# Two modulation sums of each feed-forward moved behind its down product, on one core

## The chip, the cores and the metric

The kernel runs on one core of one Trainium2 chip. The metric is the device time of one execution in microseconds (us), as the median of several runs. PE is TensorE, DVE is VectorE, ACT is ScalarE, POOL is GpSimd, SP is SyncE; PEld is PE's loading of weights.

## What is computed

Two transformer blocks of two layers each over 256 tokens of width 1024, all in float32. Cut to what matters here:

```python
def first_block(x, ...):
    for i in range(2):
        h = rms_norm(x, norm_mix_w[i])
        ...                                       # i = 0: gated delta rule; i = 1: nsa attention
        x = x + concatenate([mix, mo]) @ w_out[i]
        x = x + conv_glu(rms_norm(x, norm_ffn_w[i]), ffn_w_up[i], ..., ffn_w_down[i])
    return rms_norm(x, final_norm_w)

def second_block(x, c, w_ada, b_ada, ...):
    cond = silu(c)
    for l in range(2):
        mod = cond @ w_ada[l] + b_ada[l]          # 1024 -> 6144
        shift1, scale1, gate1, shift2, scale2, gate2 = split(mod, 6)
        h = rms_norm_2(x, norm1_g[l]) * (1 + scale1) + shift1
        ...                                       # mLSTM and attention mixers
        x = x + gate1 * (merged @ w_out[l])
        h2 = rms_norm_2(x, norm2_g[l]) * (1 + scale2) + shift2
        x = x + gate2 * hierarchical_moe(h2, ...) # 32 experts
```

The modulations `mod` of the second block depend on `c` alone, so they can be made while the first block runs. Each of the two layers has 12 chunks of 512 columns; the kernel numbers them 0 to 23.

## The kernel before

**Engines and order.** Every engine has its own program, written out by hand as a function (`sync`, `tensor`, `vector`, `scalar`, `gpsimd`), in which `gdn`, `project_out(0)`, `ffn(0)`, `nsa`, `project_out(1)`, `ffn(1)`, and twice `mixers` and `moe` follow one another. An engine runs its program in that order; semaphores tie the engines together.

**Weights.** SP asks for weight blocks of 2 MB (some of 1 MB) in a fixed order. They go to `wring`, a ring `W` of five places (more in the expert stage). A request waits until the block that held its place before has been freed, and those behind it wait too. Around each down product SP's order is: down block, chunk 3 (or 18), down block, chunk 4 (19), down block, chunks 5 and 6 (20 and 21), down block, chunks 7 and 8 (22 and 23), and two last down blocks; then the blocks of the next stage. With five places, the place of chunk 7 goes to the second block of the next stage and that of chunk 8 to the third, which in the first feed-forward is chunk 9 (`ADA_NSA`, line 526). The first block of the next stage takes the place of the down block ahead of them.

**One modulation chunk.** `ada_chunk` (VectorE, L120 and L129) multiplies the block's eight tiles by `silu(c)` and adds them up in the block's first tile, in eight instructions. `ada_sum` (PE, L106) adds over the 128 partitions by one product of 128x512 with a matrix of ones (tiles `ps<-wring,CS`; two records in the trace) into a bank of the ring `PB`, and frees the weight place. `ada_out` (VectorE) takes the result out of the bank and frees it: four instructions for a scale (L125, L137, L129, L125), three for a shift, one for a gate (L125, `AR<-ps,AR`). Chunks 7 and 8 are a half of `scale2` and a half of `shift1`; 22 and 23 are the halves of layer 1's `gate2`.

**Banks.** PSUM has eight banks: the ring `PA` is `ps0` to `ps3`, the ring `PB` is `ps4` to `ps7`. `bank` takes the next place of a ring in turn and waits until what was in it has been read.

**The down product.** `down` (line 718) makes 256x1024 results in four banks of `PA` (token half m, column half c). Five groups of weight blocks follow one another, the last made of two blocks; PE waits for both before it starts it. Behind each of the first four groups stands what `between` gives, here the sums of `ADA_DOWN`:

```python
    ADA_DOWN = [[(3,), (4,), (5, 6), (7, 8)], [(18,), (19,), (20, 21), (22, 23)]]
```

**The norm behind it.** VectorE adds each result to X (`add_x`), makes the statistics of each token half with ACT's help and writes XN (`norm_part`). PE transposes XN by halves (`norm_half`, L109: four transposes into each of two banks of `PB`). The scaled transposes go to HT: the first token half by ACT alone, of the second half four features by VectorE (`norm_features`) and four by ACT. In the first feed-forward ACT scales a half as soon as it is there (`norm_ends`); in the second it first makes the roots of two norms for both halves, since a final norm of the first block lies between, and then scales both halves. Only then `features` (PE) multiplies the next stage's weights with HT.

In the first feed-forward the transposes of token half 0 stand inside `down`, ahead of its last quarter (`then` is "nsa"), and those of half 1 at the start of `nsa`. In the second one both stand at the start of `mixers(0)` (lines 1230 and 1231 before).

Of the kernel before, what the change touches and what calls it, by code (L numbers as in the profile page):

```python
# [294 lines left out]
def build(nc, t, out):  # L295
# [98 lines left out]
    G = at(10752, 22, 256)  # L394
# [130 lines left out]
    ADA_DOWN = [[(3,), (4,), (5, 6), (7, 8)], [(18,), (19,), (20, 21), (22, 23)]]  # L525
# [148 lines left out]
    def tensor(e):  # L674
# [43 lines left out]
        def down(done, tag, srcs, lhs, between=(), then=None, ready=(), halfway=None):  # L718


            groups = [[x] for x in srcs[:-2]] + [srcs[-2:]]
            for n, group in enumerate(groups):
                held = [(weights(name, kt, 1024), k0, kt) for name, k0, kt in group]
                final = n == len(groups) - 1
                for m in range(2):
                    if n == 0 and m and halfway:
                        halfway()
                    for c in range(2):
                        if n == 0:
                            bank(e, PA, (tag, m, c))  # L730
                        if final and m and c and then:
                            norm_half(then, 0)
                        for i, (wt, k0, kt) in enumerate(held):
                            if ready:
                                e.wait_ge(*ready[n + i])
                            for k in range(kt):
                                ins = e.matmul(PA[tag, m, c][:, :], lhs[:, k0 + k, tok(m)], wt[:, k, c * 512:c * 512 + 512],
                                               n == 0 and i == 0 and k == 0, final and i == len(held) - 1 and k == kt - 1)
                        if final:
                            ins.then_inc(done, (tag, m, c))  # L740
                if not final:
                    ins.then_inc(done, (tag, "group", n))
                for name, _, _ in group:
                    W.free(name, (done, (tag, 1, 1) if final else (tag, "group", n)))
                if n < len(between):
                    between[n]()
# [310 lines left out]
        def ffn(layer):  # L1057

            done, vect = sig("ffn_mm"), sig("ffn_v")
            tag = ("ffn", layer)  # L1060

            def product(i, part):
                name, nb = up_name(layer, i), up_blocks(i)
                a11, a12, a21, a22, total = up_tiles(layer, i)
                if part == 1:
                    bank(e, PB, ("p1", name))
                    place(name)
                    lhs, rhs, to = a11, HT[:, 0:4, tok(0)], (PB["p1", name], 0)
                    e.wait_ge(sig("norm_ha"), (tag, 0, 3))
                elif part == 2:  # L1070
                    bank(e, PA, ("p26", name))
                    lhs, rhs, to = a12, HT[:, 4:8, tok(0)], (PA["p26", name], 0)
                    e.wait_ge(sig("norm_ha"), (tag, 0, 7))
                elif part == 7:
                    bank(e, PA, ("p57", name))
                    lhs, rhs, to = a21, TS[2], (PA["p57", name], nb)
                    e.wait_ge(vect, ("t", layer, 2))
                    e.wait_ge(vect, ("s3", name))
                elif part == 5:
                    lhs, rhs, to = total, TS[0], (PA["p57", name], 0)  # L1080
                    e.wait_ge(vect, ("t", layer, 0))
                    e.wait_ge(vect, ("s1", name))
                elif part == 6:
                    lhs, rhs, to = a11, TS[1], (PA["p26", name], nb)
                    e.wait_ge(vect, ("t", layer, 1))
                    e.wait_ge(vect, ("s2", name))
                elif part == 3:
                    bank(e, PA, ("p34", name))
                    lhs, rhs, to = a12, HT[:, 4:8, tok(1)], (PA["p34", name], 0)
                    e.wait_ge(sig("norm_ha"), (tag, 1, 7))  # L1090
                    e.wait_ge(vect, ("s4", name))
                else:
                    lhs, rhs, to = a22, TS[3], (PA["p34", name], nb)
                    e.wait_ge(vect, ("t", layer, 3))
                ps, b0 = to
                for b in range(nb):
                    for k in range(4):
                        c = 128 * (b0 + b)
                        ins = e.matmul(ps[:, c:c + 128], lhs[:, k, 128 * b:128 * b + 128], rhs[:, k, :], k == 0, k == 3)
                ins.then_inc(done, (name, part))  # L1100
                if part == 4:
                    W.free(name, (done, (name, 4)))
                elif part == 5:
                    SUMS.free(name, (done, (name, 5)))

            product(0, 1)
            product(0, 2)
            norm_half(tag, 1)
            for i, part in ((1, 1), (1, 2), (0, 7), (0, 5), (0, 6), (0, 3), (0, 4), (1, 7), (1, 5), (1, 6)):
                product(i, part)  # L1110
            PA.defer()
            product(1, 3)
            product(1, 4)
            for i in range(2, 12):
                for part in (1, 2, 7, 5, 6, 3, 4):
                    product(i, part)
                if i - 1 in ADA_UP[layer]:
                    ada_sum(ADA_UP[layer][i - 1])

            srcs = [(("down", layer, j), 4 * (j - 1) if j else 20, 4 if j else 2) for j in DOWNS]  # L1120
            ready = [(vect, ("val", layer, j - 1 if j else 5)) for j in DOWNS]
            down(done, tag, srcs, G, [lambda ns=ns: [ada_sum(n) for n in ns] for ns in ADA_DOWN[layer]],
                 None if layer else "nsa", ready)

        def nsa():
            done, vect, act = sig("nsa_mm"), sig("nsa_v"), sig("nsa_a")
# [100 lines left out]
        def mixers(layer):  # L1227
            done, vect, act = sig(f"mix_mm{layer}"), sig(f"mix_v{layer}"), sig(f"mix_a{layer}")
            tag = ("mix", layer)
            norm_half(tag, 0)  # L1230
            norm_half(tag, 1)
            for ch in range(2):
                name = (f"qk{ch}", layer)
# [348 lines left out]
    def vector(v):  # L1582
# [409 lines left out]
        def ffn(layer):  # L1992
            done, mm, act = sig("ffn_v"), sig("ffn_mm"), sig("ffn_a")
            tag = ("ffn", layer)
# [97 lines left out]
            for n in range(first, last + 2):  # L2092
                if n <= last:
                    ada_chunk(n)
                if n > first:
                    ada_out(n - 1)
            for m in add_x(mm, tag, done):
                if layer:
# [3 lines left out]
                    norm_part("nsa", m)  # L2102
            if layer == 0:
                norm_features("nsa")

        def last_part(tag, m):
            r, f = norm_scale(tag, m)
# [94 lines left out]
        def mixers(layer):  # L2202
            done, mm, act = sig(f"mix_v{layer}"), sig(f"mix_mm{layer}"), sig(f"mix_a{layer}")
            tag = ("mix", layer)
            norm_features(tag)
            RAW, E, S3 = mixer_rings(layer)
            lg, e1, neg, nb, cb = (sm((n, layer), 2, 8) for n in ("lg", "me1", "neg", "nb", "cb"))
            halves = lambda x: x.rearrange("p a (b c) -> p a b c", b=2)
# [998 lines left out]
```

## Time and profile before

| what | value |
|---|---|
| median of 3 runs | 2495.95 us (2493.03 to 2497.18) |
| the profiled execution | 2493.57 us |
| its span, first to last instruction | 2491.8 us |
| PE busy | 2239.1 us (90%) |
| DVE busy | 1085.4 us (44%) |
| ACT busy | 588.3 us (24%) |
| DMA, mean rate | 261 GB/s |
| mean granted clock of PE | 0.958 |

The profile shows one execution. Times in it count from the start of its span. PE's busy time overlaps from one matmul to the next, and the ends of matmuls are modelled; where PE waits is read from the idle time ahead of a row. The first feed-forward's down product runs from 502 to 586 us, the second's from 980 to 1064 us; the experts of the second block run from about 1320 on, with a mixer stage of the second layer between 1780 and 2025.

### The profile page before, as it was taken

To read this page: it belongs to the slowest core of one execution; us is meant where nothing else is said; L and a number is where in the kernel's file an instruction comes from. 1 tells how busy PE (TensorE), PEld (TensorE's weight loads), DVE (VectorE), ACT (ScalarE), POOL (GpSimd) and SP (SyncE) were. 2 spreads that over 40 slices of the span, in tenths; PEclk is the share of its full clock that TensorE was granted. 3 is DMA by queue.
4 is the path that set the end of the run, shared out by engine and by line. 5 is a ranking of instruction groups with operands and counts; after the bars stand their busy time and mean duration, and the time that the engine had idled before them with its cause. 6 is when DMAs were issued, how large, how long until landed. Compare 5 with 4: busy or idle time off the path is not lost.

```text
span 2491.8 us, 31934 instructions
## 1 busy us (share of the span) xinstructions
PE 2239.1 (90%) x12996; PEld 1463.1 (59%) x12996; DVE 1085.4 (44%) x2397; ACT 588.3 (24%) x1304; POOL 58.4 (2%) x88
## 2 busy tenths in 40 slices
PE   8999999899989999999998977877899989887886
PEld 7888879846865798467763433333568744333332
DVE  4764458873464787543433222222324342222222
ACT  4331423001143220032522111111214421111111
POOL 0010000001000000002000000000002000000000
PEclk9999999999999999999998999999899989999998
DMA  7221234586932645835248999999743369999996
GB/s 277 102 77 68 102 133 169 189 335 193 318 123 99 223 170 210 330 130 169 102 184 361 427 428 427 427 428 427 294 150 115 158 264 427 427 427 427 427 427 286
DMA packets 140910, 651.37 MB, mean 261 GB/s; under 512 B 6971, under 2 KB 13419, under 8 KB 116049
## 3 DMA queue, kind: packets, MB, share of 16 engines
q1 hardware_dynamic: 138336, 642.19, 65.4%
q0 software_dynamic: 2416, 7.02, 1.2%
q8 instruction: 106, 1.74, 0.3%
q14 instruction: 52, 0.42, 0.0%
HBM read 647.88 MB, written 1.31 MB: 261 GB/s over the span
## 4 chain that ended last, share of the span: by engine, by line
PE 62%; DMA 23%; DVE 10%; ACT 3%; issue 2%; DVEq 0%; ACTq 0%
PE ps L106 60%; DMA wring<-in_w_up 13%; DMA AR<-in_w_up 8%; DVE AR L125 2%; PE ps L109 2%; DVE AR L129 2%; DMA wring<-in_ffn_w_down 1%; DVE wring L129 1%; ACT AR L115 1%; DVE wring L125 1%; ACT L115 1%; DVE AR L120 1%; ACT HT L115 1%; DVE AR L133 0%; ACT wring L115 0%
## 5 line engine op out<-in xcount | busy, mean ns | idle before, releaser
L106 PE MATMUL ps<-HT,wring 128*128 128x256 f32 (+1 forms) x2848 | 533.6, 346 | 10.7 <-DVE wring L125 9.2
L106 PEld LDWEIGHTS ps<-HT,wring 128*128 128x128 f32 x2848 | 468.5, 194 | 68.1 <-DVE wring L125 11.0
L106 PE MATMUL ps<-wring,AR 128*32 128x512 f32 (+3 forms) x1344 | 338.1, 599 | 18.1 <-DVE AR L125 14.1
L106 PE MATMUL ps<-wring,MN 128*32 128x512 f32 (+1 forms) x1408 | 220.7, 636 | 59.5 <-DMA wring<-in_w_up 39.2
L115 ACT ACTIVATE AR<-ps 128x128 f32<-128x128 f32 (+6 forms) x234 | 94.5, 404 | 719.5 <-PE ps L106 663.1
L106 PEld LDWEIGHTS ps<-wring,AR 128*32 128x32 f32 (+1 forms) x1344 | 132.6, 149 | 176.4 <-issue 173.6
L106 PE MATMUL ps<-AR 128*128 128x128 f32 (+7 forms) x1432 | 204.6, 416 | 15.5 <-DVE AR L125 13.1
L125 DVE TENSOR_TENSOR AR<-ps,AR 128x512 f32<-128x512 f32 (+4 forms) x200 | 100.6, 503 | 264.5 <-ACT AR L115 165.3
L106 PEld LDWEIGHTS ps<-wring,MN 128*32 128x32 f32 (+1 forms) x1408 | 65.3, 122 | 210.9 <-issue 100.3
L141 DVE COPY HT<-ps 128x512 f32<-128x512 f32 x64 | 44.3, 692 | 326.2 <-PE ps L106 326.2
L106 PEld LDWEIGHTS ps<-AR 128*128 128x128 f32 (+5 forms) x1432 | 139.2, 173 | 54.7 <-issue 41.7
L106 PE MATMUL ps<-AR,MN 128*32 128x512 f32 (+1 forms) x800 | 107.7, 650 | 45.5 <-DMA AR<-in_w_up 40.5
L106 PEld LDWEIGHTS ps<-CS,HT 128*128 128x128 f32 x1024 | 119.1, 191 | 48.9 <-issue 48.9
L115 ACT ACTIVATE HT<-ps 128x512 f32<-128x512 f32 x112 | 66.9, 597 | 311.8 <-PE ps L106 310.3
L106 PE MATMUL ps<-XN,wring 128*128 128x128 f32 x1056 | 133.3, 280 | 6.3 <-DVE wring L125 6.3
L106 PEld LDWEIGHTS ps<-XN,wring 128*128 128x128 f32 x1056 | 126.9, 196 | 6.9 <-DVE wring L125 6.8
L129 DVE SCALAR_TENSOR_TENSOR wring<-wring,CC 128x512 f32<-128x512 f32 x168 | 126.3, 752 | 6.0
L106 PE MATMUL ps<-CS,HT 128*128 128x32 f32 x1024 | 126.2, 277 | 0.0
L106 PE MATMUL ps<-XN,AR 128*128 128x128 f32 (+1 forms) x656 | 114.2, 414 | 1.6 <-DVE AR L137 1.6
L106 PEld LDWEIGHTS ps<-AR,MN 128*32 128x32 f32 (+1 forms) x800 | 28.5, 120 | 116.7 <-DMA AR<-in_w_up 56.8
L125 DVE TENSOR_TENSOR MN<-ps,AR 128x512 f32<-128x512 f32 x64 | 44.3, 692 | 119.4 <-PE ps L106 119.4
L115 ACT ACT_TABLE_LOAD x66 | 84.7, 1283 | 13.2 <-issue 5.1
(172 smaller groups left out, 2140.7 us busy)
## 6 DMA issues: line engine op xcount, KB each, us to landing
wring<-in_w_gate SPq DMA_DIRECT2D x40, 2048.0 KB, 37.1
wring<-in_w_up SPq DMA_DIRECT2D x40, 2048.0 KB, 32.0
wring<-in_w_down SPq DMA_DIRECT2D x40, 2048.0 KB, 35.2
wring<-in_w_ada SPq DMA_DIRECT2D x24, 2048.0 KB, 8.5
AR<-in_w_down SPq DMA_DIRECT2D x24, 2048.0 KB, 35.2
AR<-in_w_gate SPq DMA_DIRECT2D x24, 2048.0 KB, 35.5
AR<-in_w_up SPq DMA_DIRECT2D x24, 2048.0 KB, 31.2
wring<-in_ffn_w_up SPq DMA_DIRECT2D x20, 2048.0 KB, 8.0
```

Source lines behind the costliest of these rows:

```text
L106: return Ins(self.eng and self.eng.matmul(out, lhs, rhs, start=start, stop=stop), None)
L109: return Ins(self.eng and self.eng.transpose(out, in_, ident), None)
L115: return Ins(self.eng and self.eng.activation(out, in_, func, **kw), self)
L120: return Ins(self.eng and self.eng.tensor_scalar(out, in_, s1, None, op0), self)
L125: return Ins(self.eng and self.eng.tensor_tensor(out, in0, in1, op), self)
L129: return Ins(self.eng and self.eng.scalar_tensor_tensor(out, in0, s, in1, op0, op1), self)
L141: return Ins(self.eng and self.eng.tensor_copy(out, in_), self)
```

## The change

The sums of the last entry of `ADA_DOWN` (chunks 7 and 8, then 22 and 23) leave the place ahead of the last group of the down product. On PE they now stand behind the whole product, in the first feed-forward ahead of the transposes of token half 1, in the second between the transposes of the two halves. On VectorE `ada_chunk` stays where it was, and `ada_out` of these chunks goes behind `norm_features` of the next stage.

```diff
@@ tensor, ffn(layer)
-            down(done, tag, srcs, G, [lambda ns=ns: [ada_sum(n) for n in ns] for ns in ADA_DOWN[layer]],
+            down(done, tag, srcs, G, [lambda ns=ns: [ada_sum(n) for n in ns] for ns in ADA_DOWN[layer][:3]],
                  None if layer else "nsa", ready)
+            if layer:
+                norm_half(("mix", 0), 0)
+            for n in ADA_DOWN[layer][3]:
+                ada_sum(n)
@@ tensor, mixers(layer)
-            norm_half(tag, 0)
+            if layer:
+                norm_half(tag, 0)
             norm_half(tag, 1)
@@ vector, ffn(layer)
-                if n > first:
+                if n > first and n - 1 not in ADA_DOWN[layer][3]:
                     ada_out(n - 1)
...
             if layer == 0:
                 norm_features("nsa")
+                late_sums(0)
+
+        def late_sums(layer):
+
+            for n in ADA_DOWN[layer][3]:
+                ada_out(n)
@@ vector, mixers(layer)
             norm_features(tag)
+            if layer == 0:
+                late_sums(1)
```

PE in the first feed-forward, before: from the sums ahead of the down product's last group to the first products of the nsa stage. `ps4` to `ps7` are the ring `PB`; `ps<-wring,CS` are the sums; `[waits ...]` names the semaphores.

```order
L106 MATMUL ps6<-wring,CS 128x512 [waits s_ada_v]
L106 MATMUL ps7<-wring,CS 128x512 [waits s_ada_v]
L106 MATMUL ps3<-wring,AR 128x512 [waits s_w2,s_w1]
...
L109 MATMUL ps4<-CS,XN 128x128 [waits s_norm_v]
...
L109 MATMUL ps5<-CS,XN 128x128 [waits s_norm_v]
...
L106 MATMUL ps2<-wring,AR 128x512 x8
L109 MATMUL ps6<-CS,XN 128x128 [waits s_norm_v,s_ada_v]
...
L109 MATMUL ps7<-CS,XN 128x128 [waits s_norm_v,s_ada_v]
...
L106 MATMUL ps4<-HT,wring 128x256 [waits s_norm_ha,s_norm_hv,s_w3]
```

The same stretch of PE in the changed kernel:

```order
L106 MATMUL ps3<-wring,AR 128x512 [waits s_w2,s_w1]
...
L109 MATMUL ps6<-CS,XN 128x128 [waits s_norm_v]
...
L109 MATMUL ps7<-CS,XN 128x128 [waits s_norm_v]
...
L106 MATMUL ps2<-wring,AR 128x512 x8
L106 MATMUL ps4<-wring,CS 128x512 [waits s_ada_v]
L106 MATMUL ps5<-wring,CS 128x512 [waits s_ada_v]
L109 MATMUL ps6<-CS,XN 128x128 [waits s_norm_ha,s_norm_v]
...
L109 MATMUL ps7<-CS,XN 128x128 [waits s_norm_ha,s_norm_v]
...
L106 MATMUL ps4<-HT,wring 128x256 [waits s_norm_hv,s_ada_v,s_w3]
```

The two sums stand behind the last quarter of the down product and hold ps4 and ps5; the first products of the nsa stage take ps4 after sum 7, and wait for s_ada_v, not for the transposes' reader.

VectorE at the same place, from the last scaling of XN on, before:

```order
L121 TENSOR_SCALAR XN<-X,SM 128x512 [waits s_norm_v] x2
L120 TENSOR_SCALAR HT<-ps6,PV 128x128 [waits s_norm_v,s_norm_mm]
L120 TENSOR_SCALAR HT<-ps6,PV 128x128 [waits s_norm_hv] x3
L120 TENSOR_SCALAR AR<-ps6 8x512 [waits s_norm_hv,s_nsa_mm]
L120 TENSOR_SCALAR wring<-wring,CC 128x512 [waits s_nsa_v,s_w0]
```

and in the changed kernel:

```order
L120 TENSOR_SCALAR HT<-ps6,PV 128x128 [waits s_norm_hv] x3
L125 TENSOR_TENSOR ps4<-ps4,CS 64x8x64 [waits s_norm_hv,s_ada_mm]
L137 TENSOR_REDUCE MC<-ps4 64x8 [waits s_ada_v]
L129 SCALAR_TENSOR_TENSOR MC<-MC,PV 64x8 [waits s_ada_v]
L125 TENSOR_TENSOR MC<-MC,PV 64x8 [waits s_ada_v]
L125 TENSOR_TENSOR ps5<-ps5,CS 128x512 [waits s_ada_v,s_ada_mm]
L137 TENSOR_REDUCE MC<-ps5 128x4 [waits s_ada_v]
L125 TENSOR_TENSOR MC<-MC,PV 128x4 [waits s_ada_v]
L120 TENSOR_SCALAR AR<-ps6 8x512 [waits s_ada_v,s_nsa_mm]
```

The seven instructions that empty ps4 and ps5 stand behind the scalings of HT, where they had been ahead of the additions to X.

PE behind the second feed-forward, before: the transposes of both token halves and the first products of the mixer stage.

```order
L109 MATMUL ps7<-CS,XN 128x128 [waits s_norm_v]
...
L109 MATMUL ps4<-CS,XN 128x128 [waits s_norm_v]
...
L109 MATMUL ps5<-CS,XN 128x128 [waits s_norm_v,s_ada_v]
...
L109 MATMUL ps6<-CS,XN 128x128 [waits s_norm_v,s_ada_v]
...
L106 MATMUL ps7<-HT,wring 128x256 [waits s_norm_ha,s_norm_hv,s_w1]
```

and in the changed kernel:

```order
L109 MATMUL ps5<-CS,XN 128x128 [waits s_norm_v]
...
L109 MATMUL ps6<-CS,XN 128x128 [waits s_norm_v]
...
L106 MATMUL ps7<-wring,CS 128x512 [waits s_ada_v]
L106 MATMUL ps4<-wring,CS 128x512 [waits s_ada_v]
L109 MATMUL ps5<-CS,XN 128x128 [waits s_norm_ha,s_norm_v]
...
L109 MATMUL ps6<-CS,XN 128x128 [waits s_norm_ha,s_norm_v]
...
L106 MATMUL ps7<-HT,wring 128x256 [waits s_norm_hv,s_ada_v,s_w1]
```

The transposes of the second half now follow those of the first in the same two banks, and wait for s_norm_ha, ACT's scalings; the first products take the bank of sum 22.

## Rows read from the trace of the kernel before

**Rows 1.** The page's part 4: the chain that ended last, shares of the span.

```profile
PE 62%; DMA 23%; DVE 10%; ACT 3%; issue 2%; DVEq 0%; ACTq 0%
```

**Rows 2.** The chain in order of time, 500 to 1160: start us, us, what.

```profile
540.06 17.02 DMA wring<-in_ffn_w_down
...
590.17 91.36 PE ps L106 x522
...
1071.45 88.64 PE ps L106 x366
```

**Rows 3.** Timeline of PE, first feed-forward: start us, us, what, [idle before].

```profile
553.60 1.02 PE L106 MATMUL ps<-wring,CS 128*128 128x512 f32 x2
555.01 1.12 PE L106 MATMUL ps<-wring,CS 128*128 128x512 f32 x2 [0.39 <-DVE wring L129]
557.21 20.84 PE L106 MATMUL ps<-wring,AR 128*128 128x512 f32 x48 [1.08 <-DMA wring<-in_ffn_w_down]
...
578.76 7.03 PE L106 MATMUL ps<-wring,AR 128*128 128x512 f32 x16
588.96 1.21 PE L109 MATMUL ps<-CS,XN 128*128 128x128 f32 x8 [3.17 <-DVE XN L121]
590.12 15.74 PE L106 MATMUL ps<-HT,wring 128*128 128x256 f32 x64
...
606.74 14.08 PE L106 MATMUL ps<-HT,wring 128*128 128x256 f32 x64
```

**Rows 4.** Timeline of DVE, first feed-forward.

```profile
555.06 0.71 DVE L125 TENSOR_TENSOR ps<-ps,CS 64x512 f32<-64x512 f32 x1
...
556.73 0.16 DVE L125 TENSOR_TENSOR MC<-MC,PV 64x8 f32<-64x8 f32 x1
...
589.62 1.51 DVE L120 TENSOR_SCALAR HT<-ps,PV 128x128 f32<-128x128 f32 x4 [0.23 <-PE ps L109]
...
607.63 0.49 DVE L120 TENSOR_SCALAR wring<-wring,CC 128x512 f32<-128x512 f32 x1
...
613.74 0.49 DVE L120 TENSOR_SCALAR wring<-wring,CC 128x512 f32<-128x512 f32 x1
```

**Rows 5.** Timeline of PE, second feed-forward.

```profile
1031.53 1.88 PE L106 MATMUL ps<-wring,CS 128*128 128x512 f32 x4
1035.16 27.70 PE L106 MATMUL ps<-wring,AR 128*128 128x512 f32 x64 [1.75 <-DMA wring<-in_ffn_w_down]
1062.70 1.04 PE L109 MATMUL ps<-CS,XN 128*128 128x128 f32 x8
1069.51 1.94 PE L109 MATMUL ps<-CS,XN 128*128 128x128 f32 x8 [5.77 <-DVE XN L121]
1071.24 15.85 PE L106 MATMUL ps<-HT,wring 128*128 128x256 f32 x64
```

**Rows 6.** Timeline of DVE, second feed-forward.

```profile
1033.45 0.69 DVE L125 TENSOR_TENSOR AR<-ps,AR 64x512 f32<-64x512 f32 x1 [0.18 <-PE ps L106]
...
1070.63 1.75 DVE L121 TENSOR_SCALAR HT<-ps,MC 128x128 f32<-128x128 f32 x4 [0.69 <-PE ps L109]
```

**Rows 7.** Timeline of ACT, second feed-forward.

```profile
1068.25 5.97 ACT L115 ACTIVATE HT<-ps,MC 128x128 f32<-128x128 f32 x12
```

**Rows 8.** Stretches: busy us (x) of PE, PEld, DVE, ACT, POOL; clock, DMA, GB/s.

```profile
590.30:593.60 3.30, 3.30 (x9) 2.59 (x9) 0.76 (x3) 1.37 (x4) 2.16 (x4) 0.50 1.05 400
593.70:597.00 3.30, 3.30 (x17) 2.91 (x16) 0.00 (x0) 0.00 (x0) 0.00 (x0) 1.00 1.06 359
1071.30:1074.90 3.60, 3.60 (x10) 2.88 (x10) 1.01 (x3) 2.69 (x6) 1.07 (x2) 0.50 0.76 247
```

**Rows 9.** Timeline of SP's requests, first feed-forward.

```profile
553.79 1.23 SPq L101 DMA_DIRECT2D wring<-in_nsa_w_in  x2
...
585.82 0.37 SPq L101 DMA_DIRECT2D wring<-in_nsa_w_in  x1
```

**Rows 10.** Waits of SP's queue, 1140 to 1400: total us, times, longest.

```profile
SPq L101 <- PE ps L106: 229.7, 28, 29.9
```

## The prediction, made before the changed kernel ran

> **What bounds the kernel now.** I read the page first: the chain that ended last is three fifths TensorE [rows 1], so a microsecond saved or lost on PE counts only where the chain runs on PE. The chain in order of time shows where that is around the change [rows 2]. In the first feed-forward it goes through the last load of down weights (17.02 us, from 540.06) and from 590.17 through 522 matmuls in a row; behind the second it takes PE again from 1071.45. A start that is late there moves all that follows. Later the experts' loads end last in the chain, but until they run without a break the SP queue waits for PE, 28 times and 229.7 us between 1140 and 1400 [rows 10]: places in the weight ring come free when PE has read them, so a late PE makes late loads. I therefore pass every PE delay on in full, and take nothing off.
>
> **In front of the last group.** PE's timeline of the first feed-forward [rows 3]: the fourth of five groups ends at about 553.6, the sums of chunks 7 and 8 run from 553.60 and 555.01 with 0.39 us of waiting for VectorE, and then PE waits 1.08 us for a load of in_ffn_w_down and starts the last group at 557.21. The chain says the same [rows 2]: 540.06 + 17.02 = 557.08 is that load, asked for when the sums of chunks 5 and 6 had freed its place. Neither moves. So with two sums fewer PE only waits longer, some 3.6 us (553.60 to 557.21). In the second feed-forward the sums run 1031.53 to 1033.4 and the last group starts at 1035.16, again behind a load [rows 5]. **Gain in front: 0.** The bounds: 0, and 3.6 + 3.6 us if the load came before PE is there. One small way to that exists: the next two weight blocks are asked for at 553.79 [rows 9], 3.3 us before the awaited load lands, and the second of them now goes out only behind the last group. Those requests stand behind the awaited one, so I take 0. The Trainium skill, page "DMA: Bandwidth & Descriptors", section "Two DMAs through the same engine are not ordered", says that within one queue of one DMA engine descriptors start in order but are pipelined and that nothing orders them across the engines; by its first half the gain is 0, by its second a fraction of a microsecond could be there. No row here separates the two.
>
> **Behind the last group, first feed-forward.** PE ends it at 585.79 (578.76 + 7.03) and stands idle 3.17 us until the second half's XN is there at 588.96 [rows 3]. Two sums are four matmul records of 512 columns, each 7.03 / 16 = 0.44 us: 1.8 us. They fit in the idle, and the transposes still start at 588.96. **Cost there: 0**, covered by VectorE's norm of the second half; without that cover it would be the 1.8 us.
>
> The bill comes at the banks. The order of PE shows it: the sums now take two of the four banks of ring PB between the norm's halves, so the first product of the nsa columns gets ps4, the bank of sum 7, and waits for s_ada_v. Before it got the bank of the first half's transposes, which ScalarE had long emptied. VectorE empties the sum's bank in `ada_out(7)`, which now stands behind `norm_features`: 4 scalings from 589.62 take 1.51 us, to 591.13 [rows 4]. `ada_out(7)` took from 555.06 to 556.73 + 0.16 = 556.89, that is 1.83 us with its four instructions, so it ends at 593.0, and PE starts 0.14 us later, at 593.14, not at 590.12 [rows 3, 4]. **+3.0 us.** `ada_out(8)` has no more instructions, so it ends at most 1.9 us later, and its bank is wanted only after half a chunk of products (15.74 / 2 = 7.9 us). VectorE's own work is not late: its next chunk starts at 607.63 [rows 4].
>
> **Second feed-forward.** The transposes of the norm's first half move from `mixers` into `ffn`, to the same place in PE's order; new are the two sums behind them. PE is free at 1063.74, the XN comes at 1069.51 [rows 5]: the sums hide again. But here the transposes of the second half now share ps5 and ps6 with those of the first, and wait for s_norm_ha. ScalarE scales the first half only from 1068.25, because it makes both halves' roots first: 12 scalings in 5.97 us, 0.497 each [rows 7], so ps5 is free at 1068.25 + 4 x 0.497 = 1070.24 and ps6 at 1072.2. The first four transposes go from 1069.51 to 1070.38. VectorE began its scalings 1.12 us after those transposes (1070.63 against 1069.51), so now 1071.5, and ends 1.75 us later [rows 6], at 1073.25. Then `ada_out(22)`, one instruction of 0.69 us [rows 6], to 1073.96; PE starts at 1074.1, not at 1071.24 [rows 5]. **+2.9 us.** ScalarE's four last scalings end near 1075.4, by when PE, at 0.49 us for a k, doesn't need them yet.
>
> **The clock.** The granted clock is 0.50 (the 1.2 GHz level) from about 590.3 to 593.6 and from 1071.3 to 1074.9, and 1.00 right behind the first stretch [rows 8]. Both followed an idle PE, 3.17 and 5.77 us, and both ended 4.7 and 5.4 us after PE's first work (588.96 to about 593.7, 1069.51 to about 1074.9). Products at the lower level cost about 3.4 / 2 = 1.7 us and 3.7 / 2 = 1.85 us. After the change the sums cut the first idle to 1.4 us, but a second one of 3 us follows the transposes, so I expect the lower level again. If the level returns 4.7 and 5.4 us after the products start, instead of after the transposes, the low stretches cost 2.35 and 2.7 us: 0.65 and 0.85 more. If it doesn't fall in the first feed-forward, 1.7 less. I take half of the 1.5: **+0.8**, since part of the earlier return was paid by the transposes; bounds -1.7 and +1.5.
>
> **Loads held back.** The place of chunk 7 goes to the second nsa block and that of chunk 8 to chunk 9. They were asked for at 553.79 and just behind it, the next pair at 585.82 [rows 9]; now all four go out from about 586.8. At 400 GB/s [rows 8] a block of 2.1 MB takes 5.2 us: they land near 592, 597, 603 and 608 with no wait between. PE wants the second block at 606.74, VectorE chunk 9 at 607.63 and chunk 10 at 613.74 [rows 3, 4], all 3 us later by now. Behind the second feed-forward the second block is wanted not before 1087.1 (1071.24 + 15.85) [rows 5]. **0**, with 5 us of cover at the tightest place.
>
> **Sum.** 0 + 3.0 + 2.9 + 0.8 = +6.7 us. Against the profiled execution (2493.57 us, its span 2491.8) that is 2500.3; the median of the three runs is 2.4 us above that execution, so I forecast 2495.95 + 6.7 = 2502.6 us. A measurement of this kernel can tell about 0.2% (5 us) from no change.
>
> **Rivals.**
> 1. *The load comes in time.* Place: the last load of down weights. If with fewer blocks behind it it landed before PE's fourth group ends, PE would gain up to 3.6 + 3.6 = 7.2 us in front, against +6.7: 2495.5, no slower than before. It decides from the point where the wait in front of the last group falls below 3.6 us. Against it: the load is asked for at the same moment, and the wait behind the sums was there in both feed-forwards. A part of it (1 to 2 us) is more likely than all: 0.08.
> 2. *The clock stays up.* The sums break the first idle, the level doesn't fall, and the second stretch costs what it did: 3.0 + 2.9 - 1.7 = +4.2, 2500.2. For it: the longest idle left is no longer than before. Against: two idles close together, with little work between them. 0.10.
> 3. *The banks cost nothing*, so the change moves only idle time: 2496. The Trainium skill, page "Perfetto Trace Analysis", section "Optimizing Tensor Performance", advises that independent matmul groups rotate through banks so that emptying one overlaps the next group's matmuls; by it the waits would be hidden. The order speaks against it: the ring has four places and comes round to the sum's bank before VectorE is at `ada_out`. 0.06.
> 4. *A held-back load is late.* If the four loads took 10 us each, chunk 10 would land near 627, 10 us late, and its sum and the third block with it: at least +5 more, 2508. For it: small loads of GpSimd share that stretch. Against: the rates of rows 8. 0.08.
>
> My forecast itself has 0.68. Its own range is +4.5 to +9; some 0.58 of the 0.68 lies above +5, with rival 4 giving 0.66 for slower. Same takes the rest of the forecast (0.10), rival 2 (0.10), and 0.10 of rivals 1 and 3. Faster is left with 0.04, the far ends of these two. The range from 2497.5 to 2507.0 leaves out the full forms of rivals 1, 3 and 4.
>
> **What would show it.** In the new profile: PE's wait of about 3.6 us in front of the last group, put down to in_ffn_w_down, with the start of the group where it was; the sums right behind the down product; the transposes of the first feed-forward not later; 522 matmuls that start 3 us later behind a wait for VectorE; in the second, transposes that wait for ScalarE's HT in two pieces and products 2.9 us later. It would be wrong if the last group starts sooner by more than 1 us, if the products behind the norm wait less than 2 us more, or if PE waits for in_nsa_w_in or in_w_ada.

## The result, and the profile of the changed kernel

The changed kernel takes 2505.86 us, the median of 6 runs (2503.11 to 2512.66), beside 2494.38 us for the kernel before in the same session (6 runs, 2490.64 to 2497.18): ratio 1.0058, 95% interval 1.0043 to 1.0073. It is 11.5 us slower by the medians (their quotient is 1.0046) and 14.5 by the ratio, with 10.7 to 18.2 in its interval, where +6.7 was forecast. The sign and both bank waits were right; what was missing is the slower last group behind a longer wait, and a further loss between the two feed-forwards.

The execution profiled of the changed kernel is the slowest of its six (2512.66 us), 6.8 us above their median and 19.1 above the profiled one of before. The two feed-forwards are set against those of before by the same landmarks in both traces; of the rest, only whole stretches are compared. The page (its first line, and part 4: shares of the chain that ended last) answers to [rows 1]:

```profile
span 2510.6 us, 31938 instructions
...
PE 64%; DMA 21%; DVE 10%; ACT 3%; issue 2%; DVEq 0%; ACTq 0%
```

PE's part of the chain grew and the transfers' part shrank: the loss sits where PE leads. PE's timeline of the first feed-forward (start us, us busy, instructions; in brackets idle time ahead and what ended it) answers to [rows 3]:

```profile
538.52 13.90 PE L106 MATMUL ps<-wring,AR 128*128 128x512 f32 x32
...
555.54 23.79 PE L106 MATMUL ps<-wring,AR 128*128 128x512 f32 x48 [3.12 <-DMA wring<-in_ffn_w_down]
579.16 1.04 PE L109 MATMUL ps<-CS,XN 128*128 128x128 f32 x8
580.03 7.03 PE L106 MATMUL ps<-wring,AR 128*128 128x512 f32 x16
586.90 1.88 PE L106 MATMUL ps<-wring,CS 128*128 128x512 f32 x4
590.23 1.21 PE L109 MATMUL ps<-CS,XN 128*128 128x128 f32 x8 [1.45 <-DVE XN L121]
...
594.45 16.31 PE L106 MATMUL ps<-HT,wring 128*128 128x256 f32 x64 [3.00 <-DVE MC L125]
611.64 14.08 PE L106 MATMUL ps<-HT,wring 128*128 128x256 f32 x64
```

The 3.00 us in front of the products is the bank wait. But the last group's first 48 records take 23.79 us, where they took 20.84. VectorE's timeline shows who held the bank (answers to [rows 4]):

```profile
590.90 1.51 DVE L120 TENSOR_SCALAR HT<-ps,PV 128x128 f32<-128x128 f32 x4 [0.23 <-PE ps L109]
...
592.51 0.71 DVE L125 TENSOR_TENSOR ps<-ps,CS 64x512 f32<-64x512 f32 x1
...
594.18 0.17 DVE L125 TENSOR_TENSOR MC<-MC,PV 64x8 f32<-64x8 f32 x1
```

It empties sum 7's bank only behind the scalings of HT, and ends at 594.35; PE starts 0.10 us later. PE's timeline of the second feed-forward (answers to [rows 5]):

```profile
1027.40 13.90 PE L106 MATMUL ps<-wring,AR 128*128 128x512 f32 x32
...
1044.83 29.40 PE L106 MATMUL ps<-wring,AR 128*128 128x512 f32 x64 [3.53 <-DMA wring<-in_ffn_w_down]
1074.07 1.04 PE L109 MATMUL ps<-CS,XN 128*128 128x128 f32 x8
1074.94 1.88 PE L106 MATMUL ps<-wring,CS 128*128 128x512 f32 x4
1081.79 1.08 PE L109 MATMUL ps<-CS,XN 128*128 128x128 f32 x4 [4.97 <-ACT HT L115]
1083.82 1.09 PE L109 MATMUL ps<-CS,XN 128*128 128x128 f32 x4 [0.94 <-ACT HT L115]
1085.56 16.51 PE L106 MATMUL ps<-HT,wring 128*128 128x256 f32 x64 [0.65 <-issue]
1101.90 3.64 PE L106 MATMUL ps<-SW,HT 128*128 128x16 f32 x32
```

The transposes wait for ScalarE's HT in two pieces. The first products then wait for sum 22's bank, which VectorE begins to empty only here:

```profile
1084.77 1.48 DVE L125 TENSOR_TENSOR AR<-ps,AR 64x512 f32<-64x512 f32 x2
```

The granted clock in stretches of the changed kernel (stretch; us; busy us of PE, PEld, DVE, ACT, POOL with counts; clock; DMA share; GB/s) answers to [rows 8]:

```profile
552.50:555.40 2.90, 0.00 (x0) 0.00 (x0) 1.08 (x2) 0.00 (x0) 0.00 (x0) 0.87 1.02 388
555.60:560.40 4.80, 4.80 (x6) 2.09 (x7) 0.00 (x0) 0.00 (x0) 0.00 (x0) 0.50 0.89 329
563.00:566.00 3.00, 3.00 (x9) 1.32 (x8) 0.37 (x1) 0.00 (x0) 0.00 (x0) 1.00 0.00 0
1045.00:1048.00 3.00, 3.00 (x6) 1.23 (x6) 0.00 (x0) 0.00 (x0) 0.00 (x0) 0.69 1.04 383
594.50:597.80 3.30, 3.30 (x8) 2.64 (x9) 1.50 (x3) 0.00 (x0) 0.00 (x0) 0.50 1.06 364
```

Behind the longer load wait PE starts the last group at 0.50, the 1.2 GHz level, and is back at 1.00 by 563. Before, with the sums inside that wait, the group started at full speed, as a stretch of the kernel before shows:

```profile
557.30:562.00 4.70, 4.70 (x11) 2.08 (x12) 1.25 (x3) 0.00 (x0) 0.00 (x0) 1.00 1.05 390
```

In the second feed-forward the changed kernel has 0.69 from 1045 to 1048 and 0.74 in the 3 us behind, where the kernel before has 1.00 from 1035.3 to 1040. The ledger between landmarks, us:

| stretch of PE | before | after | difference |
|---|---|---|---|
| first feed-forward: fourth group to last group | 17.34 | 17.02 | -0.32 |
| last group to transposes of token half 2 | 31.75 | 34.69 | **+2.94** |
| transposes to first nsa products | 1.16 | 4.22 | +3.06 |
| products to the second nsa block | 16.62 | 17.19 | +0.57 |
| second feed-forward: fourth group to last group | 17.37 | 17.43 | +0.06 |
| last group to transposes of half 1 | 27.54 | 29.24 | **+1.70** |
| transposes of half 1 to first products | 8.54 | 11.49 | +2.95 |
| products to the small products (128x16) | 15.69 | 16.34 | +0.65 |
| sum | | | +11.6 |

The sum lies within the interval and at the 11.5 of the medians, but it isn't all that the change costs: of the 19.1 us between the two profiled executions it leaves 7.5 elsewhere, 4.7 of them between the two feed-forwards, where the old kernel's work is unchanged. 11.6 and 4.7 make 16.3, which lies in the interval too. So that 11.6 meets the medians doesn't show that nothing else was lost. The 4.7 us: from the second nsa block to the second feed-forward's fourth group it takes 415.76 us, before 411.05. A piece of the same work in both, the changed kernel's stretch first and then that of before:

```profile
690.00:695.00 5.00, 3.89 (x16) 3.33 (x17) 1.40 (x8) 4.54 (x10) 0.00 (x0) 0.62 0.78 285
```

```profile
685.00:690.00 5.00, 3.68 (x22) 3.04 (x23) 2.15 (x13) 4.54 (x9) 0.00 (x0) 1.00 0.77 281
```

Over the next 5 us the clock is 0.70 against 1.00: the level fell here too, 100 us behind the change, and in these 10 us alone 3.4 us of clock are missing. The three kernels whose first feed-forward is as before (the old one, and two of the experiments below) take 411.05, 411.00 and 411.02 us between the feed-forwards; the other eight take 412.2 to 423.7. So an edit in the first feed-forward shows again in this stretch, through the clock as here, in some kernels through waits for loads.

Below, S1 is the sum of the first four lines (66.87 before, 73.12 after), S2 of the last four (69.14 and 74.50).

### The profile page after: what moved, and what is told of

Its sections match the earlier page's. It is cut to its first block, busy times and chain, and to the rows that moved or that the text cites. A ratio compares the mean times of both kernels' runs of the same rounds, so it can differ in the third digit from the quotient of the medians.

```text
span 2510.6 us, 31938 instructions
## 1 busy us (share of the span) xinstructions
PE 2254.3 (90%) x12996; PEld 1471.2 (59%) x12996; DVE 1085.5 (43%) x2397; ACT 588.8 (23%) x1304; POOL 58.4 (2%) x88
## 3 DMA queue, kind: packets, MB, share of 16 engines
q8 instruction: 107, 1.75, 0.3%
## 4 chain that ended last, share of the span: by engine, by line
PE 64%; DMA 21%; DVE 10%; ACT 3%; issue 2%; DVEq 0%; ACTq 0%
PE ps L106 61%; DMA wring<-in_w_up 10%; DMA AR<-in_w_up 9%; DVE AR L125 2%; PE ps L109 2%; DVE AR L129 2%; DMA wring<-in_ffn_w_down 1%; DVE wring L129 1%; ACT AR L115 1%; DVE wring L125 1%; ACT HT L115 1%; ACT L115 1%; DVE AR L120 1%; DVE AR L133 0%; ACT MN L115 0%
## 5 line engine op out<-in xcount | busy, mean ns | idle before, releaser
L106 PE MATMUL ps<-AR 128*128 128x128 f32 (+7 forms) x1432 | 209.4, 424 | 15.2 <-DVE AR L125 12.6
```

Source lines behind the costliest of these rows:

```text
L106: return Ins(self.eng and self.eng.matmul(out, lhs, rhs, start=start, stop=stop), None)
```

## The experiments

Theory: two bank waits of 3 us, and the clock level lost in the last groups. Rivals: the clock follows the new waits behind the norm; the loads that are now asked for late; something elsewhere in the kernel. The kernel before ran again beside each set of experiments, and each median stands beside its own.

**Banks.** The moved sums go to the ring `PA`, idle there, so that no product or transpose comes round to their bank.

```diff
+    LATE = (7, 8, 22, 23)
...
-            ps = bank(e, PB, ("ada", n))
+            ps = bank(e, PA if n in LATE else PB, ("ada", n))
```

> The changed kernel, with the four moved sums in banks of the ring PA, which the down product has just left, instead of PB. Theory: the waits behind the norm come from the ring PB, so the first products of the next stage start behind the transposes again: 3.0 us back in the first feed-forward, and 2.9 us in the second, where the transposes of the second half no longer wait for ScalarE; the slower last group stays. Against the kernel before: +5.5 us (2 to 8). Rival: the waits come from VectorE's later ada_out wherever the sums lie, or from the load traffic that moved there; then the products still start 3 us late and the time stays at +11.5 us.

Measured: 2498.49 against 2491.81 us, ratio 1.0033 [1.0022, 1.0044]. S1 67.77, S2 70.54. PE's timeline of this kernel:

```profile
553.79 23.66 PE L106 MATMUL ps<-wring,AR 128*128 128x512 f32 x48 [3.26 <-DMA wring<-in_ffn_w_down]
...
588.27 1.24 PE L109 MATMUL ps<-CS,XN 128*128 128x128 f32 x8 [1.36 <-DVE XN L121]
589.46 14.05 PE L106 MATMUL ps<-HT,wring 128*128 128x256 f32 x64
...
651.47 1.94 PE L106 MATMUL ps<-wring,CS 128*128 128x512 f32 x2 [3.65 <-DVE MC L125]
```

Both bank waits are gone, and with the first one the low clock behind it; S1 falls by 5.35, S2 by 3.96 (the block behind the small products then takes 1.7 back: 15.75 us, before 14.06). The last group stays slow: its clock has nothing to do with the banks. The time is within the expected range by the medians, and just above it by the ratio (8.2 us). The 0.9 and 1.4 us left in S1 and S2 don't make up the 6.7 us of the medians; between the feed-forwards it takes 416.68 us, 5.6 more than before, and 3.65 of that is the last row, a new wait: VectorE is late with chunk 11's sum. VectorE's timeline, and the chain at the same place (start us, us, what), show what it waits for:

```profile
643.50 0.48 DVE L120 TENSOR_SCALAR wring<-wring,CC 128x512 f32<-128x512 f32 x1 [4.99 <-DMA wring<-in_w_ada]
```

```profile
618.51 24.96 DMA wring<-in_w_ada
```

A load of 2 MB takes 25 us. The stretches of the same kernel, around the place where the held-back loads run and where GpSimd's transfers of bias_rows join them:

```profile
598.00:604.00 6.00, 6.00 (x28) 4.61 (x26) 0.00 (x0) 0.42 (x2) 0.00 (x0) 1.00 1.04 384
622.00:628.00 6.00, 6.00 (x29) 5.30 (x28) 0.16 (x1) 0.77 (x2) 0.00 (x0) 1.00 1.03 164
```

and of the kernel before:

```profile
598.00:604.00 6.00, 6.00 (x30) 5.28 (x29) 0.00 (x0) 0.77 (x2) 0.00 (x0) 1.00 0.18 63
622.00:628.00 6.00, 6.00 (x30) 5.28 (x29) 1.27 (x3) 0.00 (x0) 2.04 (x4) 1.00 1.03 158
```

Before, the share over 598 to 604 was 0.18, with little left to load, so the loads had a start on the slow stretch; here it still runs at full share. That this head start is what is missing is read from the rows; no run moved it alone. In the changed kernel itself VectorE takes chunk 11 at 645.87 without a wait: the late loads are covered by the other delays, and come out when these are mended. The Trainium skill, "Perfetto Trace Analysis", section "DMA Optimizations", says that transfers under 2 KB have significant overhead each. From 612 to 645 us only 308 of the 3634 packets of the kernel with the sums in `PA` are under 2 KB, so that rule doesn't explain 164 GB/s; what does stays open.

**Work in front.** The changed kernel, with two useless products of 512 columns ahead of each last group, where the sums had been. They add work to the kernel; their output is never read.

```diff
+        def busy(n):
+            i = PB.order[0]
+            for s, key in PB.freed.get(PB.held[i], ()):
+                e.wait_ge(s, key)
+            for _ in range(n):
+                e.matmul(PB.places[i][:, :], ONES, CS[:, 0:512], True, True)
...
-            down(done, tag, srcs, G, [lambda ns=ns: [ada_sum(n) for n in ns] for ns in ADA_DOWN[layer][:3]],
+            down(done, tag, srcs, G, [lambda ns=ns: [ada_sum(n) for n in ns] for ns in ADA_DOWN[layer][:3]] + [lambda: busy(2)],
```

> The changed kernel, with two products without use (a matrix of ones times constants, into the next bank of PB, never read) where the two sums had been, ahead of the last group of both down products. They only keep PE at work for 1.7 us of the wait for the load. Theory: the last group ran slower (23.79 against 20.84 us for 48 records, 29.40 against 27.70 for 64) because PE had stood idle and its granted clock had fallen; so both groups take 20.9 and 27.7 us again, and the time is 4.6 us below the changed kernel: +7 us (4 to 9) against before. Rival: the group is slowed by something that the change did to the loads or banks (the next weight block asked for later); then both stay at 23.8 and 29.4 us and the time at +11.5 us.

Measured: 2498.86 against 2491.81 us, ratio 1.0036 [1.0023, 1.0049]. S1 69.84, S2 74.57. PE's timeline of this kernel:

```profile
551.40 1.88 PE L106 MATMUL ps<-CS 128*128 128x512 f32 x4
...
554.93 20.84 PE L106 MATMUL ps<-wring,AR 128*128 128x512 f32 x48 [1.65 <-DMA wring<-in_ffn_w_down]
...
590.89 15.74 PE L106 MATMUL ps<-HT,wring 128*128 128x256 f32 x64 [3.00 <-DVE MC L125]
...
1037.22 29.40 PE L106 MATMUL ps<-wring,AR 128*128 128x512 f32 x64 [1.95 <-DMA wring<-in_ffn_w_down]
```

In the first feed-forward 1.88 us of work that computes nothing give back 23.79 - 20.84 = 2.95 us, with the clock at 1.00 from 555 to 560: the term that the prediction lacked, on its own. Its bank wait stays at 3.00, which rules out that the one hangs on the other. In the second the group is as slow as without the products, though the idle is 1.95 us and not 3.53: this half of the expectation failed. The time is in the expected range all the same: 7.05 us by the medians, 9.0 by the ratio.

**Both.**

```diff
-            ps = bank(e, PB, ("ada", n))
+            ps = bank(e, PA if n in LATE else PB, ("ada", n))
...
-            down(done, tag, srcs, G, [lambda ns=ns: [ada_sum(n) for n in ns] for ns in ADA_DOWN[layer][:3]],
+            down(done, tag, srcs, G, [lambda ns=ns: [ada_sum(n) for n in ns] for ns in ADA_DOWN[layer][:3]] + [lambda: busy(2)],
```

> The edits of the two kernels ahead of this one together: the moved sums in PA, and two products without use where they had been. Theory: the two causes (bank waits 5.9 us, clock in the last group 4.6 us) are apart and add up to all of the loss but the clock behind the norm; so 0 to +1.5 us against before, and down to -2 if the sums behind the product also keep the clock up. Rival: something third, such as the later requests for weight blocks, costs several us; then +3 us or more is left.

Measured: 2497.13 against 2491.81 us (12 runs, 2491.32 to 2505.27), ratio 1.0023 [1.0010, 1.0035]. S1 65.10, S2 68.39, less than before in both. PE's timeline of this kernel:

```profile
554.71 20.84 PE L106 MATMUL ps<-wring,AR 128*128 128x512 f32 x48 [1.71 <-DMA wring<-in_ffn_w_down]
587.56 14.05 PE L106 MATMUL ps<-HT,wring 128*128 128x256 f32 x64
...
649.98 2.08 PE L106 MATMUL ps<-wring,CS 128*128 128x512 f32 x2 [4.07 <-DVE MC L125]
...
1043.47 27.70 PE L106 MATMUL ps<-wring,AR 128*128 128x512 f32 x64 [1.70 <-DMA wring<-in_ffn_w_down]
```

Both terms are gone, and here the second feed-forward's last group is back at 27.70 us too. Yet the kernel isn't as fast as before, and the rival's case holds (+3 us or more is left): between the feed-forwards this execution takes 423.67 us, 12.6 more than before. 4.07 of these are the wait for chunk 11, and the clock from 675 to 805 is 0.89, where it was 0.95. The execution is 4.2 us above its kernel's median, so not all of it is in the time above.

**The kernel before, with work in the norm's idle.** Three useless products ahead of the transposes of half 2 in the first feed-forward, six behind the second (`busy` as above).

```diff
+            busy(3)
             norm_half("nsa", 1)
...
             norm_half(tag, 0)
+            if layer == 0:
+                busy(6)
             norm_half(tag, 1)
```

> The kernel before, with products without use in PE's wait for the second half's XN: three (2.6 us) in the first feed-forward, six (5.2 us) in the second. Nothing else moves. Theory: the granted clock falls behind these waits, and costs 1.7 us in the first and 0.9 + 1.85 us in the second; with PE at work it stays at 1.00 and the time is 4.4 us below before (-2 to -6). Rival: the products behind the norm are slow for another reason (they start before ScalarE has scaled HT, or the loads), then no change, or +1 us if the products without use delay the transposes.

Measured: 2492.16 against 2491.81 us, ratio 1.0007 [0.9997, 1.0016]. S1 65.01, S2 67.26: 1.86 and 1.88 us less, where 1.7 and 2.75 were expected. The time was to fall by 4.4 us and doesn't: that missed. Behind them, PE's timeline of this kernel:

```profile
1085.68 4.38 PE L106 MATMUL ps<-SW,HT 128*128 128x16 f32 x32
1089.90 16.68 PE L106 MATMUL ps<-HT,wring 128*128 128x256 f32 x64
```

Before, these took 3.64 and 14.06 us: the clock now falls during the small products (0.84 over 1090 to 1106), and takes back 3.4 us, more than was won behind the second feed-forward. The same holds for the first: between the feed-forwards this kernel takes 416.04 us, 5.0 more than before, with 0.89 from 675 to 805. A filler only moved the place at which the level is lost.

**One feed-forward at a time.** The change for layer 0 alone, and for layer 1 alone:

```diff
 # first only, beside the kernel before
+            for n in () if layer else ADA_DOWN[layer][3]:
+                ada_sum(n)
...
 # second only, beside the changed kernel
-            for n in ADA_DOWN[layer][3]:
+            for n in ADA_DOWN[layer][3] if layer else ():
```

> The change in the first feed-forward alone (chunks 7 and 8); the second is as before. Theory: this half costs the idle ahead of the last group (2.9 us of slow clock), the bank wait (3.0) and 0.6 behind it: from the fourth group's start to the second block's products 73.1 us, against 66.9 before; +6 us in time (3 to 9). Rival: the halves aren't separate, and one of them holds nearly all of the 11.5 us; then this is under +3 or over +9.

Measured: 2502.83 against 2490.68 us, ratio 1.0043 [1.0030, 1.0056]. S1 73.28, S2 69.67.

> The change in the second feed-forward alone (chunks 22 and 23); the first is as before. Theory: 1.7 us of slow clock in the last group, 2.9 of bank waits and 0.7 behind them: from the fourth group's start to the small products behind the first block 74.5 us, against 69.1 before; +5.4 us (3 to 8). Rival: as in the run ahead, under +2.5 or over +8.

Measured: 2494.44 against 2490.68 us (2489.79 to 2501.01), ratio 1.0016 [1.0007, 1.0025]. S1 66.63, S2 75.45. The last groups in PE's timeline, of the change in the first alone:

```profile
559.87 23.68 PE L106 MATMUL ps<-wring,AR 128*128 128x512 f32 x48 [3.44 <-DMA wring<-in_ffn_w_down]
...
1049.02 29.40 PE L106 MATMUL ps<-wring,AR 128*128 128x512 f32 x64 [1.91 <-DMA wring<-in_ffn_w_down]
```

and of the change in the second alone:

```profile
553.93 20.84 PE L106 MATMUL ps<-wring,AR 128*128 128x512 f32 x48 [0.84 <-DMA wring<-in_ffn_w_down]
...
1031.69 30.59 PE L106 MATMUL ps<-wring,AR 128*128 128x512 f32 x64 [3.35 <-DMA wring<-in_ffn_w_down]
```

S1 grows by 6.4 with the change in the first, S2 by 6.3 with that in the second, and each stays near its old value without it. The two ratios add up to 0.59%, the whole change to 0.58%: the halves add up. In time the first half lies above its expected range (3 to 9), with 12.2 us by the medians and 10.7 by the ratio: 6.4 us of it are S1, and 4.6 more lie between the feed-forwards, where it takes 415.68 us, as the changed kernel does (415.76), and 411.00 with the second half alone. The second half costs 3.8 us by the medians and 6.3 by its trace. The runs of one kernel spread over up to 16 us, and I don't read that difference further. The row at 1049.02 matters: with the sums in front, as in the kernel before, and 1.91 us of waiting the level was lost too.

**The loads.** With the sums moved, nothing wants the two chunk blocks ahead of the last down blocks any more. SP asks for the down blocks first; the sums use `PA`.

```diff
@@ sync, ffn(layer)
-                for a in ADA_DOWN[layer][g] if g < 4 else ():
+                for a in ADA_DOWN[layer][g] if g < 3 else ():
                     ada(a)
+            for a in ADA_DOWN[layer][3]:
+                ada(a)
```

> The changed kernel with the moved sums in banks of PA, and with the weight blocks of the four chunks asked for behind the last two down blocks, not ahead of them. Theory: PE's wait ahead of the last group was for the last down block behind two chunk blocks in the queue; it goes (3.6 us in each feed-forward sooner than in the changed kernel), and with it the slow clock in the last group: the last group starts within 0.3 us of the fourth's end and takes 20.8 and 27.7 us. In the first feed-forward the second block of the next stage and the three behind it still go out only behind the product, and chunk 11 is late again, 4 to 5 us: -3 us against before (-6 to +1). Rival: VectorE, which gets chunks 7, 8, 22 and 23 later, becomes late with the norm, and nothing is won: 0 to +4.

Measured: 2484.90 against 2490.68 us, ratio 0.9979 [0.9968, 0.9990]. S1 61.44, S2 65.13. PE's timeline of this kernel:

```profile
536.83 34.50 PE L106 MATMUL ps<-wring,AR 128*128 128x512 f32 x80
...
583.33 14.05 PE L106 MATMUL ps<-HT,wring 128*128 128x256 f32 x64
...
642.84 1.13 PE L106 MATMUL ps<-wring,CS 128*128 128x512 f32 x2 [1.15 <-DVE MC L125]
...
1011.97 41.36 PE L106 MATMUL ps<-wring,AR 128*128 128x512 f32 x96
```

The fourth and the last group run as one, with no wait and at the full level. The time is within the expected range. S1 and S2 lose 5.4 and 4.0 us, 9.4 together, of which 5.8 arrive. Between the feed-forwards it takes 413.70 us, 2.7 more than before, with 1.15 for chunk 11 in it (4 to 5 were expected); the remainder isn't placed.

**The loads, in the second feed-forward only.** The first as before; bank, order and loads changed for layer 1 (`LATE = (22, 23)`).

> The first feed-forward as before. In the second the sums stand behind the product in banks of PA, and the blocks of chunks 22 and 23 are asked for behind the last two down blocks. Theory: the wait of 3.6 us ahead of the last group goes, nothing is added behind it, and no load of the mixer stage is late, since its first use is 20 us away: -4 us against before (-6 to -2). Rival: held-back loads of the mixer stage are late as chunk 11 was in the first; then 0 to +3, with PE or VectorE waiting for in_w_in.

Measured: 2485.48 against 2490.68 us (10 runs, 2483.30 to 2487.85), ratio 0.9975 [0.9966, 0.9984]. S1 66.69, S2 65.64; its last two groups take 41.36 us for 96 records without a wait, as above. All of the gain of both feed-forwards together comes with the second alone: 3.5 us in S2, 5.2 in the time. The two intervals overlap, so the two kernels can't be told apart in time; this one needs the smaller edit.

**The loads with fillers.** The version with the loads moved in both feed-forwards, with one and four useless products in the norm's idle.

```diff
+            busy(1)
             norm_half("nsa", 1)
...
             if layer:
                 norm_half(tag, 0)
+            else:
+                busy(4)
             norm_half(tag, 1)
```

> The run e7_loads (moved sums in PA, chunk blocks asked for behind the down blocks) with products without use behind the moved sums, in the rest of PE's wait for the norm: one (0.9 us) in the first feed-forward, four (3.5 us) in the second. Theory: in the second the level of PE's clock stays up, which gives 0.9 us in the transposes and up to 1.8 in the first block's products; the fill kernel e4 took 67.3 us there against 69.1. Against before: -6 to -9 us. Rival: what the clock keeps here it loses in the next stretch with little work (e4 lost it at the next block, 16.68 us for 64 records against 14.06), so the same time as e7_loads within 1.5 us.

Measured: 2486.43 against 2491.83 us, ratio 0.9980 [0.9968, 0.9993]. S1 61.44, S2 63.68, the latter 1.45 us shorter, but the block behind it takes 15.75 us and PE waits 3.7 us for a chunk. No gain: the rival's case, as with the fillers in the kernel before.

## Why the prediction was wrong, step by step

1. **In front of the last group, the step that failed.** The prediction put it: "with two sums fewer PE only waits longer", "Gain in front: 0", and no cost. The timing was right: the group starts 17.02 us behind the fourth one's start, not 17.34, and waits 3.12 and 3.53 us for its load. But the idle it lengthened, from 1.08 and 1.75 us, was the one in which the sums had kept the clock up. The group then ran 2.94 and 1.70 us longer. In the first feed-forward the cause is shown: useless products in the same place gave the 2.95 back, and the group took 20.84 us in all six kernels with work there and 23.7 to 23.8 in all three that only waited. In the second the rows show the clock (0.69 and 0.74), but not that the moved sums alone cost the 1.70: with useless products there the group took 29.40 us in one kernel and 27.70 in another, and with the sums left in place 29.40 in one of three. The three kernels that only waited there took 29.40 to 30.6. The prediction read the granted clock only behind the norm, where it already fell, and not at the wait it was about to lengthen to 3.6 us. The Trainium skill, "Perfetto Trace Analysis", section "Matmul Optimizations", says that TensorE's power follows its utilization, so that matmuls should run back to back; the trace agrees, with 20.84 against 23.79 us for the same 48 records.
2. **Bank wait, first feed-forward: +3.0.** Measured +3.06; taking the sums out of the ring removes it.
3. **Bank wait, second: +2.9.** Measured +2.95, and by the path that was worked out: the transposes wait in two pieces behind ScalarE, 4.97 and 0.94 us, and then the products wait for VectorE, which empties sum 22's bank only from 1084.77 (PE's 0.65 us, which the timeline calls issue). The same run removes it.
4. **Clock behind the norm: +0.8.** Measured 0.57 + 0.65 = 1.2, within its bounds. Rival 2 (the level stays up) is out: 594.50 to 597.80 ran at 0.50.
5. **Loads held back: 0.** True of the time of this kernel, but not with "5 us of cover". The landings were worked out at 400 GB/s, and the stretch from 622 to 628 carries 158 to 164. With the other delays removed, VectorE waited up to 3.2 us for chunk 10, which cost PE nothing, and up to 5.4 for chunk 11, which cost PE 1.2 to 4.1. Rival 4 was thus real, behind the others.
6. **Rivals 1 and 3.** The load didn't come in time: the wait grew by 2.0 and 1.8 us. The banks cost what was said. The load would have come in time had its order been changed too, which the change didn't do.
7. **Between the feed-forwards: no term.** Measured +4.7, with the level falling at 690 us. The prediction looked for the clock only beside the changed places.

In sum: 3.1 + 2.9 where 3.0 + 2.9 was put, 1.2 instead of 0.8, 4.6 for which there was no term, less 0.3 in front of the last group: 11.6 against 6.7, and 4.7 more between the feed-forwards. The range ended 11.05 us above the old median, short of the measured difference by medians and by ratio.

What stays open: why the level falls at 690 us in the changed kernel and not before, with the same waits ahead of the same small products. It falls there in four of the eleven kernels, and among them is the old one with fillers, so the moved sums aren't needed for it. The rest of the 7.5 us lies outside the places above: 1.35 less ahead of the first feed-forward's fourth group and 3.8 more behind the second one's small products; over the eleven profiled executions these two parts vary by 6 and by 8 us, and not with the edits. And whether the late chunk 11 alone takes what the mended feed-forwards give wasn't tried by itself.

## What to carry to other kernels

Small work inside a wait can be what keeps TensorE's clock up: before taking it out, read the granted clock behind that wait, and price the next batch at the lower level. When a product's accumulator is moved within a ring of banks, read whose reader frees the bank that the *next* user gets. When work is moved later, move its operand's load later too: with the sums moved and their banks mended the kernel stood at +0.33%, and moving the four loads as well brought it to -0.21%. And set the unchanged stretches beside each other as well: a part of this loss lay 100 us behind the edit.

## What the runs showed of the hardware that was not expected

- What the lost clock level costs doesn't follow the length of the wait ahead. In the second feed-forward the last group took 27.70 us behind waits of 1.62 to 1.75 us, 29.40 behind 1.91 and 1.95, again 29.40 behind 3.53, but 30.6 behind 3.32 and 3.35.
- Filling an idle stretch moves the fall rather than avoiding it, and it moves without fillers too. Behind the second norm the first block took 14.4 to 14.5 us in four kernels, two of them with fillers, and then the block behind the small products of 16 columns took 15.75 to 16.68; in the other seven the first took 15.5 to 16.3 and that block 14.06. No kernel had both fast.
- The full share of the DMA engines (1.03 and 1.04) went with 384 GB/s and with 164 GB/s: the share alone doesn't say how fast a load will land. Chunk 11's 2 MB took 25 us there.
